# Moving three pieces of a two-block transformer kernel: the attention output norm, a gate's take, the first convolution

## The reference, cut to what matters

```python
h = rmsnorm(x, norm_mix_g);  proj = h @ w_in   # q, k, v, xr, gr, g_attn, g_rnn
# attention, 8 heads: q, k normed; two softmaxes per head, p0 - lam * p1, times v
out = rmsnorm(out, subln_g) * (1 - lambda_init)     # per head, over its 128 values
# recurrent branch, 8 chunks of 128 channels
xc = conv_b + sum(xpad[:, tap:tap+S] * conv_w[tap] for tap in range(4))
r, i = sigmoid(xc @ w_a + b_a), sigmoid(xc @ w_x + b_x)
a = exp(-8 * r * softplus(-lru_lambda));  b = sqrt(1 - a*a) * i * xc
hs = scan(h = a * h + b);  rnn_out = hs * gelu(gr)
merged = sigmoid(g_attn) * (attn_out @ w_proj_attn) + sigmoid(g_rnn) * (rnn_out @ w_proj_rnn)
x = x + merged @ w_out;  x = x + relu(rmsnorm(x) @ w_up)**2 @ w_down
```

## Time and profile before

| | |
|---|---|
| median of 3 runs (lowest, highest) | 2058.53 us (2057.5, 2059.64) |
| the profiled execution: its own time, its span | 2057.48 us, 2055.7 us |
| PE busy | 1951.7 us, 95% of the span |
| POOL, DVE, ACT busy | 1237.3, 1080.3, 501.0 us (60, 53, 24%) |
| DMA | 177.39 MB, mean 86 GB/s |
| chain that ended last, by engine | PE 74%, DVE 20%, ACT 3%, issue 3% |
| granted TensorE clock, mean | 0.984 |

### The profile page before, as it was taken

How to read it: one execution, slowest core, us unless ns; L and a number is a source line. 1 busy time by engine, 2 the same in 40 slices (tenths; PEclk the granted TensorE clock), 3 DMA queues, 4 the chain that set the end, 5 groups by cost and what they waited for, 6 DMA issues and landing times.

```text
span 2055.7 us, 23472 instructions
## 1 busy us (share of the span) xinstructions
PE 1951.7 (95%) x9015; PEld 1598.3 (78%) x9015; DVE 1080.3 (53%) x1516; ACT 501.0 (24%) x1001; POOL 1237.3 (60%) x1018
## 2 busy tenths in 40 slices
PE   6888887999999999999999999999999899999997
PEld 4666666888888888888878777888778788888886
DVE  7666657999355231226876686333555473223134
ACT  4444443333122010112133333010222221001012
POOL 6233325788776776766633444676767567677662
PEclk8999998999999999999999999999999999999998
DMA  5122112333333333333322322333433233333321
GB/s 158 47 62 62 49 34 75 89 89 113 103 93 92 103 92 97 98 94 101 93 52 52 77 62 67 103 93 92 123 93 103 75 100 93 98 96 94 102 78 56
DMA packets 341169, 177.39 MB, mean 86 GB/s; under 512 B 14453, under 2 KB 338203, under 8 KB 341060
## 3 DMA queue, kind: packets, MB, share of 16 engines
q1 hardware_dynamic: 339044, 173.28, 29.3%
q10 hardware_dynamic: 2016, 2.62, 0.6%
HBM read 173.75 MB, written 2.13 MB: 86 GB/s over the span
## 4 chain that ended last, share of the span: by engine, by line
PE 74%; DVE 20%; ACT 3%; issue 3%; DMA 0%; ACTq 0%; SPq 0%; DVEq 0%
PE bank L649 21%; PE bank L653 21%; PE bank L651 21%; PE bank L767 2%; PE bank L744 1%; DVE aPR L1613 1%; PE bank L715 1%; DVE fPR L1878 1%; DVE aPR L1615 1%; DVE IT L1713 1%; DVE XC L1694 1%; DVE HS L1723 1%; DVE HS L1724 1%; DVE aPR L1605 1%; PE bank L733 1%
## 5 line engine op out<-in xcount | busy, mean ns | idle before, releaser
L618 POOL TENSOR_TENSOR WL<-RAW,WH 128x1024 fp32r<-128x1024 f32 (+3 forms) x331 | 813.1, 2457 | 27.7
L649 PE MATMUL bank<-HH,WH 128*128 128x512 f32 x1560 | 623.2, 399 | 9.3 <-DVE SQ L1573 7.4
L653 PE MATMUL bank<-HH,WL 128*128 128x512 f32 x1560 | 618.8, 397 | 0.0
L651 PE MATMUL bank<-HL,WH 128*128 128x512 f32 x1560 | 615.6, 395 | 0.0
L614 POOL TENSOR_TENSOR gate<-gate 128x1 f32<-128x1 f32 x331 | 86.6, 262 | 758.8 <-PE bank L653 710.3
L649 PEld LDWEIGHTS bank<-HH,WH 128*128 128x128 f32 x1560 | 296.0, 190 | 75.1 <-issue 16.8
L615 POOL TENSOR_SCALAR WH<-RAW 128x1024 fp32r<-128x1024 f32 (+3 forms) x331 | 342.8, 1036 | 0.9 <-issue 0.2
L653 PEld LDWEIGHTS bank<-HH,WL 128*128 128x128 f32 x1560 | 296.0, 190 | 60.4 <-issue 1.7
L651 PEld LDWEIGHTS bank<-HL,WH 128*128 128x128 f32 x1560 | 296.1, 190 | 60.2 <-issue 3.4
L1764 DVE TENSOR_TENSOR X<-X,bank 128x512 f32<-128x512 f32 x80 | 55.0, 687 | 200.6 <-PE bank L653 200.6
L1486 DVE SCALAR_TENSOR_TENSOR HL<-X,PARAM,HH 128x512 fp32r<-128x512 f32 x40 | 90.8, 2269 | 30.0 <-ACT HH L1091 30.0
(11 more groups left out here) (397 smaller groups left out, 3188.0 us busy)
## 6 DMA issues: line engine op xcount, KB each, us to landing
RAW<-in_w_in SPq DMA_DIRECT2D x107, 512.0 KB, 3.7
RAW<-in_w_up SPq DMA_DIRECT2D x32, 512.0 KB, 3.9
RAW<-in_w_down SPq DMA_DIRECT2D x32, 512.0 KB, 3.9
RAW<-in_w_ffn_gate SPq DMA_DIRECT2D x22, 512.0 KB, 3.6
RAW<-in_w_ffn_up SPq DMA_DIRECT2D x22, 512.0 KB, 3.7
RAW<-in_w_xkv SPq DMA_DIRECT2D x16, 512.0 KB, 3.8
RAW<-in_w_ffn_down SPq DMA_DIRECT2D x16, 512.0 KB, 3.5
RAW<-in_w_proj_attn SPq DMA_DIRECT2D x8, 512.0 KB, 3.9
```

Source lines behind the costliest of these rows:

```text
L618: nc.gpsimd.tensor_tensor(WL[:, s, 0:k, :], RAW[:, s, 0:k, :], WH[:, s, 0:k, :].bitcast(F32), ALU.subtract).then_inc(S_[f"unit_cut{s}"], 1)
L649: mm(psum[s][:, 0:n], WH[:, s, k, :], hi(k), start=(k == 0), stop=False)
L651: mm(psum[s][:, 0:n], WH[:, s, k, :], lo(k), start=False, stop=False)
L653: last = mm(psum[s][:, 0:n], WL[:, s, k, :], hi(k), start=False, stop=(k == tiles - 1))
```

## The change

- `attend` has a new argument `late`, called after score 1 and its share of steps. In heads 1 to 7 it does the previous head's PE sum of squares (`out_stat1(h - 1)`). Only head 7's own sum still stands at the end of its head.
- ACT: the Ln and Exp of the previous head follow the Exp of t = 2, the copy to `AO[0]` that of t = 4. The squaring stays at the head's end.
- DVE: the multiply 1674 of the previous head comes in `between(1)`, behind the take of q; the subtraction 1678 in `between(2)`, behind combine(1).
- Last head: chunk 0's convolution is issued right after the copy of `OUTB`, ahead of and mixed with head 7's norm, on DVE and ACT.
- `rnn` on DVE: the take of unit 2 stands before the next chunk's convolution for n = 0, directly after it for n = 1 to 6, and before line 1718 in the last chunk. It stood behind line 1724.

```diff
@@ attend (PE)
+                    if t == 1 and late:
+                        late()
@@ head1 (PE)
-                pe.wait_ge(S_["a_o_sq"], h + 1)
-                stat("a", 3 * h + (2 if last else 4), ones[:], M1["SQ"][:, 2, :])
+                       late=(lambda: out_stat1(h - 1, 3 * h + 1)) if h else None)
+                if last:
+                    out_stat1(h, 3 * h + 2)
+            def out_stat1(h, n):
+                pe.wait_ge(S_["a_o_sq"], h + 1)
+                stat("a", n, ones[:], M1["SQ"][:, 2, :])
@@ head1 (ACT)
+                def after(t):
+                    if t == 2 and h:
+                        rsqrt_stat("a", 3 * h + 1, 1.0 / P, M1["RQ"][:, 2, :])
+                    if t == 4 and h:
+                        out_hi1(h - 1)
+                    if t == 5 and not last:
+                        square1(h + 1, 0)
...
-                rsqrt_stat("a", 3 * h + (2 if last else 4), 1.0 / P, M1["RQ"][:, 2, :])
+                if last:
+                    rsqrt_stat("a", 3 * h + 2, 1.0 / P, M1["RQ"][:, 2, :])
+                    conv_hi(0)
+                    out_hi1(h)
@@ head1 (DVE)
                     if i == 1 and not last:
                         take_qk1(h + 1, 0)
+                    if i == 1 and h:
+                        out_norm1(h - 1, 3 * h + 2)
+                    if i == 2 and h:
+                        out_lo1(h - 1)
...
+                if last:
+                    dve.wait_ge(S_["a_qk_lo"], 24)
+                    own.link(V.memset(XR[:, 0:3], 0.0))
+                    conv1_raw(0, ("first", 0, 0))
+                    out_norm1(h, 3 * h + 3)
+                    conv1_lo(0)
+                    out_lo1(h)
@@ rnn (DVE)
+                if n == 0:
+                    take(*rnn_unit(0, 2), scaled(GA))
                 if not last:
                     conv1(n + 1, ("rnn", n, 1))
+                if n:
+                    take(*rnn_unit(n, 1 if last else 2), scaled(GA))
...
                 dve.wait_ge(S_["ro_raw"], n + 1)
-                take(*rnn_unit(n, 1 if last else 2), scaled(GA))
                 dve.wait_ge(S_["ro_hi"], n + 1)
```

More of the change, by code:

```diff
@@ L748, in values, with attend @@
                     last.then_inc(S_[tag + "_pv"], 1)
-            def attend(tag, M, kind, h, steps, share, add_bias=None, stats=None):
+            def attend(tag, M, kind, h, steps, share, add_bias=None, stats=None, late=None):
                 J = len(kind.jobs)
@@ L822, in head1 @@
                 attend("a", M1, KIND1, h, steps, (2, 8, 8, 3) if last else (5, 10, 10, 2),
-                       stats=None if last else lambda side: qk_stat1(h + 1, 3 * h + 2, side))
+                       stats=None if last else lambda side: qk_stat1(h + 1, 3 * h + 2, side),
+                       late=(lambda: out_stat1(h - 1, 3 * h + 1)) if h else None)
+                if last:
+                    out_stat1(h, 3 * h + 2)
+            def out_stat1(h, n):
                 pe.wait_ge(S_["a_o_sq"], h + 1)
-                stat("a", 3 * h + (2 if last else 4), ones[:], M1["SQ"][:, 2, :])
+                stat("a", n, ones[:], M1["SQ"][:, 2, :])
             for h in range(0, HEADS - 1):
@@ L1176, in v_hi @@
                       ).then_inc(S_["a_v_hi"], 1)
-                exps("a", M1, KIND1, h, v_hi, None if last else lambda t: square1(h + 1, 0) if t == 5 else None)
+                def after(t):
[5 more added lines that the diff above has]
+                        square1(h + 1, 0)
+                exps("a", M1, KIND1, h, v_hi, after)
                 if not last:
@@ L1191, in head1, with conv_hi, out_hi1 @@
                 A(M1["SQ"][:, 2, :], M1["OR"][:], ACT.Square).then_inc(S_["a_o_sq"], 1)
-                rsqrt_stat("a", 3 * h + (2 if last else 4), 1.0 / P, M1["RQ"][:, 2, :])
+                if last:
+                    rsqrt_stat("a", 3 * h + 2, 1.0 / P, M1["RQ"][:, 2, :])
+                    conv_hi(0)
+                    out_hi1(h)
+            def conv_hi(n):
+                act.wait_ge(S_["xc_raw"], n + 1)
+                A(XCH[:], XC[:], ACT.Copy).then_inc(S_["xc_hi"], 1)
+            def out_hi1(h):
                 act.wait_ge(S_["a_o_norm"], h + 1)
@@ L1198, in _ @@
             head1(HEADS - 1, True)
-            def conv_hi(n):
-                act.wait_ge(S_["xc_raw"], n + 1)
-                A(XCH[:], XC[:], ACT.Copy).then_inc(S_["xc_hi"], 1)
             def rnn_unit(n, j):
@@ L1235, in rnn @@
                 A(SG, GA, ACT.Tanh, scale=0.5).then_inc(S_["sg"], 1)
-            conv_hi(0)
             for n in range(DC):
@@ L1671, in head1, with conv1_raw @@
                     take("qkv", h + 1, 2, scaled(M1["VR"][:]))
[L1672 to L1687, removed]
+                if last:
[5 more added lines that the diff above has]
+                    out_lo1(h)
+            def conv1_raw(n, unit):
                 take(*unit, lambda bank: V.tensor_tensor(XR[:, 3:S + 3], bank[:], RSTD[:], ALU.mult))
@@ L1698, in conv1, with conv1_lo, out_norm1, out_lo1 @@
                 ins.then_inc(S_["xc_raw"], 1)
+            def conv1_lo(n):
                 dve.wait_ge(S_["xc_hi"], n + 1)
                 V.tensor_tensor(XCL[:], XC[:], XCH[:].bitcast(F32), ALU.subtract).then_inc(S_["xc_lo"], 1)
+            def conv1(n, unit):
+                conv1_raw(n, unit)
+                conv1_lo(n)
+            def out_norm1(h, n):
+                dve.wait_ge(S_["a_stat_read"], n)
+                V.scalar_tensor_tensor(M1["OR"][:], M1["OR"][:], small[:, SUBL:SUBL + 1], M1["RQ"][:, 2, :],
+                                       ALU.mult, ALU.mult).then_inc(S_["a_o_norm"], 1)
+            def out_lo1(h):
+                dve.wait_ge(S_["a_o_norm"], h + 1)
+                dve.wait_ge(S_["a_o_hi"], h + 1)
+                V.tensor_tensor(AO[1][:, bass.ds(h, 1), :], M1["OR"][:].unsqueeze(1),
+                                AO[0][:, bass.ds(h, 1), :].bitcast(F32), ALU.subtract).then_inc(S_["a_o_lo"], 1)
+            for h in range(0, HEADS - 1):
+                head1(h, False)
+            head1(HEADS - 1, True)
             def rnn(n, last):
@@ L1742, in _ @@
             dve.sem_inc(S_["gate_i_taken"], 1)
-            dve.wait_ge(S_["a_qk_lo"], 24)
-            own.link(V.memset(XR[:, 0:3], 0.0))
-            conv1(0, ("first", 0, 0))
             for n in range(DC):
```

## The result

The changed kernel takes 2046.4 us (2044.8 to 2048.4, 4 runs) against 2058.0 (2055.9 to 2059.6, 4 runs) of the kernel before: 11.6 us less by the medians, ratio 0.9945 [0.9927, 0.9962]. 2043.5 was forecast. The profiled execution took 2048.4; its span is 2046.6.

What follows compares the result with a forecast made beforehand. PE was taken as the bound, filled in the recurrence but stalling in heads and handover. Gains 6.1 + 1.7 + 0 + 6.6 = 14.4 off 2057.5 gave 2043.1, set at 2043.5 us between profile and median; range 2034 to 2056.

Steps and rivals of the forecast that it cites:

- The heads: Norm moved into the next head's scores: period 30.65 instead of 31.44, six times, plus the first boundary: 6.1 us gained.
- tail: In each head, from the end of combine(3) to the last product: 10.8 us, as before.
- 10.2 - 1.45 + 0.85 = 9.6: Heads 1 to 6, score 0 to the take of q: stalls and refill of 1.45 go, the sum adds 0.85.
- the clock's rival: At the heads' transposes PE waits 1.9 and its clock falls, costing 11.4 over six heads: 2055; chance 0.08.
- Head 7: Last head: combine(3) 16.4 after score 0, 2.4 gained, less 0.7 for PE's falling clock: net 1.7 us.
- Part 2: Chunk 0's convolution issued earlier, at the last head's end: worth 0, between -0.5 and +0.3 us.
- The first take: Chunk 0's take ahead of the convolution: unit 1 ends 8.4 earlier, a new 1.8 stall leaves 6.6 us.
- Chunks 1 to 7: Earlier take in the later recurrent chunks: PE filled, DVE loses nothing; 0, with -3 us if DVE falls behind.
- DVE bounds the recurrence: Recurrent stage: DVE's order against POOL changes; 1 more per chunk costs PE 4 to 7 us: 2049; chance 0.09.
- The slower rival: Heads' combine(3) slips behind `WH` and `WL`: 2.75 more per head plus clock falls of about 1.9: 2071; chance 0.07.
- Better meetings: In the heads the last SCALAR_TENSOR_TENSOR gets in ahead of POOL: 0.9 more in each of six, 2038; chance 0.18.

Runs made afterwards that it cites:

- the take behind the scan: Changed kernel, but in chunks 1 to 7 unit 2's take is back behind the scan and last multiply; chunk 0 keeps its early take: 2042.0 us, ratio 0.9922.
- the subtraction later: Changed kernel with the output norm's subtraction moved out of `between(2)` to between the next head's query and key norms: 2032.1 us, ratio 0.9877.
- the first take only: Kernel before, with only chunk 0's take of unit 2 moved ahead of the next chunk's convolution: 2053.1 us, ratio 0.9975.

## Why the prediction was right, and where its terms were off

- **The heads** (6.1 in the sum): the mechanism as forecast, the size not. Per boundary 1.6 came, not 0.8; over seven 11.3. By the parts of the period: to the take 9.0 (9.6 forecast), take to combine(3) 10.1 (10.25), tail 10.7 (10.8). The mis-sized terms are the stalls, which I took from the brackets. These begin at the modelled end of a matmul, which lies behind the start of the next one where PE is filled (0.40 long, one every 0.23); from start to start a stall costs more. Two rows of the kernel before around score 0 of the next head, and two around score 2:
```profile
149.91 0.40 PE L653 MATMUL bank<-HH,WL 128*128 128x512 f32 x1
...
151.79 0.27 PE L767 MATMUL bank<-aQL,aQH 128*128 128x128 f32 x1
...
154.90 0.39 PE L649 MATMUL bank<-HH,WH 128*128 128x512 f32 x1
...
156.61 0.28 PE L767 MATMUL bank<-aQL,aQH 128*128 128x256 f32 x1
```
The boundary took 1.88 (149.91 to 151.79) and takes 0.29 (148.78 to 149.07): 1.6, where 1.3 was forecast. Score 2 came 1.71 behind the last filler step and score 3 0.78; without a wait or a sum that distance is 0.35 (154.58 to 154.93 in the changed kernel). So these two stalls cost 1.8, where "10.2 - 1.45 + 0.85 = 9.6" has 1.45. The sum of squares in its new place costs 0.86 (152.21 to 153.42, less 0.35), as forecast. The multiply took 1.25 (1.3 forecast), the stall before the transposes was 1.67 (1.9), and the clock was 1.00, so that the clock's rival did not come.
- **Head 7** (1.7): combine(3) ended 16.0 after score 0 (16.4 forecast), PE idled 4.5 and the clock fell (0.82 over 275 to 294 us). 2.5 gained, 1.2 given back on the way to the gates: 1.3.
- **Part 2** (0): right, by its own run.
- **The first take** (6.6): right. Gates' stall 5.1 (4.7), then 1.39 to 2.05 (1.8); alone 6.0.
- **Chunks 1 to 7** (0, bound -3): the step that failed, beyond its bound. "In exchange the take moves ahead of an instruction that was stretched to 2.8 by POOL, which swallows 0.69" holds only in the period of 23.1 (there that instruction takes 2.28 behind the take, in the period of 24.1 it takes 1.08). I read DVE's row in the kernel before, where chunk 0's take had held PE for 7.44 us, and did not ask where POOL's cuts go once PE runs ahead: onto the convolution. That cost 5.3 in the profile (stage 189.4 against 184.1 with the take behind the scan), though not in every execution: in the profile of the same kernel that fell into the other period the stage was 185.3. "DVE bounds the recurrence" was the rival with this mechanism, and its price of 4 to 7 is what came.
- The two errors are of about the same size, +5.2 and -5.3, so that the time came out within 3 us of the forecast by luck. It is right as a number more than as a sum.
- **The slower rival**: it exists. It did not come in the changed kernel, which missed it by some 0.5 us (TENSOR_SCALAR at 165.96, `WH` at 166.52). Putting one multiply ahead of the take instead of behind it brought it, at 4.3 per head (34.1 less 29.8; 2.75 + 1.9 forecast) and 2066 (2071 forecast). *Better meetings* exists too, and is the subtraction later.

The Trainium skill's rule (SBUF — State Buffer, section "Who interferes with whom"), that the one issued first keeps the port and the other is fully blocked, agrees with the three placements: combine(3)'s TENSOR_SCALAR takes 0.55 or 1.30, its last instruction 0.75, 1.56 or 2.71. Which it is goes with the start of POOL's gate instruction, which PE releases: 0.18 ahead of the TENSOR_SCALAR with the multiply ahead, 0.30 behind its start in the changed kernel, 0.92 behind with the subtraction later. The gate is held as well: 0.29 and 0.47 in the last two, 0.19 in the first.

## What to carry to other kernels

Where two engines hold each other up and each of their meetings is all or nothing, read the distance to the next meeting in the trace, and put an added instruction where that distance is large: the same multiply and subtraction made 2066, 2046 or 2032. When a wait is taken away from the engine that bounds a loop, ask not only what it waits for next, but where in the other engines' loop the work that it releases will fall. And run the same kernel twice before explaining a period: one profile of a loop that feeds itself shows one of its periods.

## What the runs showed of the hardware

- One kernel has two steady periods in its recurrence, 23.12 and 24.12 us, each kept to the end of the stage (five and four periods). Which one came went with the granted clock over the 6 us behind one stall, in seven profiles: 1.00 four times, with 24.1, and 0.72 three times, with 23.1. The 0.72 is the mean of eight or nine matmuls at half clock (1.2 GHz; 0.43 us from one to the next) and the rest at full clock (2.4 GHz; 0.23). The execution whose clock fell was the quicker one, 185.3 against 189.4.
- The idle time just before did not decide the clock alone. At that stall it was 0.72 after 1.99 and 2.04 us, and 1.00 after 1.39 to 1.71, but also after 2.05 with the first take only. Before the transposes of head 7 PE kept its clock after 2.11 us with the subtraction later (1.00 over 266 to 286 us), while the kernel before lost it after 2.12, with stalls of 2.45 and 0.85 just before.
